# Opening of a two-layer decoder kernel: zero matmuls, order of the first norm, blocks of the model dimension, the leading tile in plain fp32

## The chip, the cores and the metric

The kernel runs as one program on one NeuronCore of a Trainium2 chip. The metric is the device time of one execution in microseconds (us), the median of several runs. TensorE (PE) multiplies matrices, VectorE (DVE) and ScalarE (ACT) do elementwise work, GpSimd (POOL) does small work, and SyncE (SP) issues most of the loads. They run side by side and meet at semaphores; each takes its own instructions in order.

## What is computed

Two pre-norm residual layers over 256 tokens of 1024 values, all in fp32. Layer 0 mixes tokens with dilated attention, layer 1 with latent attention; each then has a mixture of experts (32 experts, two for a token) and a gated embedding:

```python
for i in range(DEPTH):                      # DEPTH = 2
    h = _rmsnorm(x, norm_mix[i])
    y = _dilated_attention(h, dsa_w_in, dsa_w_out) if i == 0 else _mla(h, ...)
    x = x + y
    x = x + _hier_moe(_rmsnorm(x, norm_moe[i]), ...)
    x = x + (p[i] @ ple_w[i]) * jax.nn.sigmoid(_rmsnorm(x, norm_ple[i]) @ ple_w_gate[i])
return _rmsnorm(x, norm_final)

# in _dilated_attention: 3 groups (dilations 1, 4, 16) x (query, key, value) x 8 heads x 128
qkv = (h @ w_in).reshape(Bn, S, DSA_GROUPS, 3, DSA_HEADS, DSA_HEAD_DIM)
```

The change lies in the first norm and in the projections of head 0, the first part of `h @ w_in`.

## The kernel before

Tokens stand in two chunks of 128 (TC = 2), the model dimension in eight blocks of 128 (KD = 8). The opening goes as follows.

- SyncE loads x chunk by chunk and the identity, then the weights of heads 0 and 1 (`load_head`, L457 to L472): for each head and each of the three groups the query and the key columns (two loads of 512 KB, the three "tiles" g = 0, 1, 2), then three loads of value columns. The first load of all counts on `first_q_in`, all others on `landed_dsa`. GpSimd loads the gains (L594) and, when tile 2 of head 0 has landed, the constants, the distances and the router (L599 to L621).
- The norm: for each chunk VectorE squares one half of x and ScalarE the other (`square`, L668 and L1024), VectorE adds (L1032), ScalarE takes the root (L678), VectorE the reciprocal (L1039), and both scale a half into `hs` (L672, L1044). PE turns `hs` block by block (`turn_rows`, L1603), VectorE multiplies by the gains on the way out of PSUM into `hT` (`gains_on`, L1055).
- The weights' rows are split as "(p k)": partition p holds the rows 8p to 8p + 7. So the k-th block of `hs` takes every eighth value of x, read with a stride.
- A product of fp32 precision is made of three single-pass matmuls: high weights by high h, high weights by low h, low weights by high h. High parts are ScalarE's casts (`high_hT` L772, `high_qk` L706, `high_v` L712), low parts VectorE's subtractions (L1146, `low_qk` L1072, `low_v` L1077). The leading tile (head 0, g = 0) is done pass by pass (L1710); all others block by block (`three_pass`, L1616 to L1618, from `project_qk` and `project_v`). Other products are plain fp32 matmuls of `pe.matmul` on fp32 operands.
- The projections go to two PSUM banks in turn (`proj_bank`): tiles 0, 1, 2, then the values of chunk 0 and of chunk 1. So the values of chunk 1 write the bank of tile 2, and `project_v` waits for its copy before that chunk (`qk_copied`, 2 + c and more).
- ScalarE's order after the high part of h is written out by hand:

```python
            high_qk(0, 1, 0, first=True)
            copy_qk(0, 0, 0, first=True)
            high_qk(0, 2, 0)
            high_v(0, 0, first=True)
            copy_qk(0, 1, 0, first=True)
            high_qk(1, 0, 1)
            copy_qk(0, 2, 0, first=True)
            high_qk(1, 1, 1)
            step(0, 1, 1, first=True)
```

`high_qk` waits for the landing of its tile, `copy_qk` (L719) for the projection. From then on `step` attends to head h while it projects head h + 1: PE does the scores (L1656), tiles 0 and 1, the transposes of the softmax (L1667), tile 2, the weighted values (L1680), the values. The loads of head h + 2 wait for the slots that head h frees; the first loads of experts wait for the slots of the last heads.

## Time and profile before

| | us |
|---|---|
| median of 3 runs | 1349.45 (1346.6 to 1352.28) |
| the profiled execution | 1347.4 |
| its span in the profile | 1345.3 |
| PE busy | 1035.3 (77%) |
| VectorE busy | 454.6 (34%) |
| ScalarE busy | 298.0 (22%) |

Times in the profile are us from the span's start, of one execution. Busy shares are means over stages with different limits. Matmuls are pipelined, so the duration of one (275 ns, say) is longer than the distance between two in a row. PE is the matmuls, PEld the weight loads beside them. L12 is line 12 of the kernel. The arrow in brackets names what ended the idle time before an instruction. In order of time a row has the start, the duration, the engine, the line, the operation and its tiles. A stretch's row has its length, the busy time and count of PE, PEld, DVE, ACT and POOL, the granted clock (1.00 is the full one), the DMA engines' share and GB/s.

### The profile page before, as it was taken

The page shows a single profiled execution, that of the slowest core. Times are in us where ns is not written, and L with a number is a line of the kernel's source. Part 1 is how long each engine was busy: PE and PEld are TensorE (multiplying, and loading weights), DVE is VectorE, ACT ScalarE, POOL GpSimd, SP SyncE. Part 2 cuts the span into 40 slices and gives each one's busy share as a digit, 9 for nine tenths or more (in the row PEclk, how much of TensorE's full clock was granted, in tenths as well). Part 3 has the DMA queues.
Part 4 walks back from the last instruction along what each step waited for, and adds up shares of the span by engine and source line. Part 5 has one row for each costly group of instructions (what it writes and reads, how often), then busy time and mean ns, then how long its engine had stood idle before and what let it go on. Part 6 is the DMA issues. An engine that isn't in the chain of part 4 may idle for free.

```text
span 1345.3 us, 31101 instructions
## 1 busy us (share of the span) xinstructions
PE 1035.3 (77%) x13816; PEld 811.3 (60%) x13816; DVE 454.6 (34%) x1005; ACT 298.0 (22%) x573; POOL 16.4 (1%) x25
## 2 busy tenths in 40 slices
PE   7999999988767666656676989988667657656667
PEld 7999999965545445444454756656444444534446
DVE  5545555562212111111212775522121111212127
ACT  5433444330100000000002754311000000000007
POOL 2000000000000000000000010000000000000000
PEclk9999999999988887888888999989788898888879
DMA  9996553599999999999999950899999999999991
GB/s 283 310 256 168 160 140 125 223 384 426 425 427 425 427 427 426 426 425 426 427 426 378 390 195 1 320 422 425 426 426 427 426 425 427 427 426 425 427 374 43
DMA packets 115817, 469.94 MB, mean 349 GB/s; under 512 B 4816, under 2 KB 79696, under 8 KB 90992
## 3 DMA queue, kind: packets, MB, share of 16 engines
q1 hardware_dynamic: 115008, 465.78, 86.8%
q8 instruction: 108, 1.77, 0.5%
q0 software_dynamic: 688, 2.28, 0.4%
q14 instruction: 13, 0.11, 0.0%
HBM read 467.00 MB, written 1.05 MB: 348 GB/s over the span
## 4 chain that ended last, share of the span: by engine, by line
DMA 52%; PE 40%; DVE 4%; ACT 2%; issue 2%; DVEq 0%; SPq 0%; ACTq 0%
DMA ring<-moe_w_down 28%; DMA ring<-moe_w_gate 13%; DMA ring<-moe_w_up 11%; PE ps L1868 6%; PE ps L1617 5%; PE ps L1618 5%; PE ps L1616 5%; PE ps L1891 4%; PE ps L1730 2%; PE ps L1755 1%; PE ps L1969 1%; PE ps L1680 1%; PE ps L1656 1%; ACT g_hi L860 1%; PE ps L1921 1%
## 5 line engine op out<-in xcount | busy, mean ns | idle before, releaser
L1868 PE MATMUL ps<-ring,scr 128*32 128x128 f32 x8192 | 284.5, 298 | 146.0 <-DMA ring<-moe_w_up 100.0
L1868 PEld LDWEIGHTS ps<-ring,scr 128*32 128x32 f32 x8192 | 247.3, 120 | 185.5 <-DMA ring<-moe_w_up 111.7
L1891 PE MATMUL ps<-ring,scr 128*32 128x256 f32 x1920 | 159.8, 487 | 117.6 <-DMA ring<-moe_w_down 105.0
L1891 PEld LDWEIGHTS ps<-ring,scr 128*32 128x32 f32 x1920 | 78.1, 134 | 180.2 <-issue 123.3
L825 ACT COPY scr<-ps 32x256 f32<-32x256 f32 x128 | 46.8, 365 | 544.9 <-PE ps L1891 544.1
L1308 DVE TENSOR_TENSOR scr<-scr,ps 128x128 f32<-128x128 f32 x64 | 23.8, 371 | 422.7 <-PE ps L1868 422.7
L1321 DVE COPY scr<-ps 32x256 f32<-32x256 f32 x128 | 53.3, 417 | 243.1 <-PE ps L1891 242.3
L1616 PE MATMUL ps<-a_hT_hi,w_qk_hi 128*128 128x256 f32 x368 | 104.4, 284 | 0.0
L1618 PE MATMUL ps<-a_hT_hi,w_qk_lo 128*128 128x256 f32 x368 | 103.8, 282 | 0.0
L1617 PE MATMUL ps<-hT_lo,w_qk_hi 128*128 128x256 f32 x368 | 103.6, 282 | 0.0
L1921 PE MATMUL ps<-scr 128*128 128x512 f32 x128 | 64.6, 651 | 15.4 <-DVE scr L1321 15.4
L818 ACT ACTIVATE scr<-ps 128x128 f32<-128x128 f32 x64 | 17.8, 278 | 260.7 <-PE ps L1868 260.7
L1755 PEld LDWEIGHTS ps<-scr,hs 128*128 128x128 f32 x512 | 61.9, 198 | 17.1 <-issue 17.1
L1616 PEld LDWEIGHTS ps<-a_hT_hi,w_qk_hi 128*128 128x128 f32 x368 | 70.0, 190 | 0.0
L1618 PEld LDWEIGHTS ps<-a_hT_hi,w_qk_lo 128*128 128x128 f32 x368 | 69.7, 190 | 0.0
L1617 PEld LDWEIGHTS ps<-hT_lo,w_qk_hi 128*128 128x128 f32 x368 | 69.7, 189 | 0.0
L1072 DVE TENSOR_TENSOR w_qk_lo<-ring,w_qk_hi 128x2048 fp32r<-128x2048 f32 x24 | 54.9, 2290 | 42.7 <-ACT w_qk_hi L706 42.7
L1755 PE MATMUL ps<-scr,hs 128*128 128x128 f32 x512 | 68.0, 287 | 0.0
L1921 PEld LDWEIGHTS ps<-scr 128*128 128x128 f32 x128 | 25.1, 207 | 52.1 <-issue 26.3
L706 ACT CAST w_qk_hi<-ring 128x2048 fp32r<-128x2048 f32 x23 | 43.9, 1909 | 8.4 <-DMA ring<-dsa_w_in 8.4
L1616 PE MATMUL ps<-w_v_hi,a_hT_hi 128*128 128x384 f32 x128 | 43.4, 339 | 0.0
L1617 PE MATMUL ps<-w_v_lo,a_hT_hi 128*128 128x384 f32 x128 | 42.8, 334 | 0.0
(283 smaller groups left out, 1195.1 us busy)
## 6 DMA issues: line engine op xcount, KB each, us to landing
ring<-moe_w_gate SPq DMA_DIRECT2D x64, 2048.0 KB, 36.5
ring<-moe_w_up SPq DMA_DIRECT2D x64, 2048.0 KB, 36.4
ring<-moe_w_down SPq DMA_DIRECT2D x60, 2048.0 KB, 36.8
ring<-dsa_w_in SPq DMA_DIRECT2D x72, 512.0 KB, 6.9
ring<-ple_w_gate SPq DMA_DIRECT2D x4, 2048.0 KB, 37.0
ring<-dsa_w_out SPq DMA_DIRECT2D x2, 2048.0 KB, 13.6
scr<-moe_w_down SPq DMA_DIRECT2D x4, 1024.0 KB, 7.3
scr<-moe_w_down SPq DMA_DIRECT2D x8, 512.0 KB, 9.5
```

The source lines that it names most:

```text
L706: act.copy(w_qk_hi[(GROUPS * par + g) % 2], w_qk[par][g]).then_inc(S("w_qk_high"), 1)
L825: ins = act.copy(e_y[CW * (i % GE):CW * (i % GE) + CW, T * q:T * q + T], bank(6)[CW * q:CW * q + CW, 0:T])
L1072: dve.tensor_tensor(w_qk_lo[par][g], w_qk[par][g], w_qk_hi[(GROUPS * par + g) % 2].bitcast(F32), ALU.subtract).then_inc(S("w_qk_low"), 1)
L1321: ins = dve.tensor_copy(e_y[CW * (i % GE):CW * (i % GE) + CW, T * q:T * q + T], bank(6)[CW * q:CW * q + CW, 0:T])
L1616: pe.matmul(dst, w_hi, x_hi, start=first, stop=False)
L1617: pe.matmul(dst, w_hi, x_lo, start=False, stop=False)
L1618: return pe.matmul(dst, w_lo, x_hi, start=False, stop=last)
L1730: mm = pe.matmul(bank(mix_bank(l, c, n)), m_o[:, k, rows], tile(Tiles.MLA_OUT + n, KD, 512)[:, k, :], start=(k == 0), stop=(k == KD - 1))
L1755: mm = pe.matmul(bank(7)[:, k * P:(k + 1) * P], hs[:, c, 4 * half + k, :], e_oneh[:, c, :], start=(c == 0), stop=(c == TC - 1))
L1868: mm = pe.matmul(bank(b)[CW * q:CW * q + CW, 0:P], xT[:, k, :], tile(t, KD, FF)[:, k, P * q:P * q + P], start=(k == 0), stop=(k == KD - 1))
L1891: mm = pe.matmul(bank(6)[CW * q:CW * q + CW, 0:T], e_hT[:, CW * j:CW * j + CW], down[j][:, T * q:T * q + T], start=(j == 0), stop=(j == FF ...
L1921: mm = pe.matmul(bank(2 * c + n), e_sc[:, c * P:(c + 1) * P], e_y[:, 512 * n:512 * n + 512], start=False, stop=True, skip_group_check=True)
```

## The change

- GpSimd first fills `warm` with zeros, and PE does 16 matmuls on it while x is loading. The waits on `fills` go up by one.
- ScalarE scales the second half of chunk 0, then squares chunk 1; it scales both halves of chunk 1. VectorE scales the first half of chunk 0 only.
- The split of the weights' rows becomes "(k p)": block k is the rows 128k to 128k + 127. The scaling reads x contiguously; the gains' layout follows.
- The product of the leading tile is one plain fp32 product of `w_qk[0][0]` and `a_hT` (h in a scratch region of its own). It waits for the gains and for the landings. Its high and low parts fall away, so the counts of `w_qk_high`, `w_qk_low` and `q_high` go down by one, in all later waits too.
- Tile 1 is done pass by pass, as the leading tile was; tile 2 block by block as before. The values of head 0 are done pass by pass over both chunks: high by high, high weights by low h, low weights by high h.

```diff
--- before.py
+++ after.py
@@ -295,6 +295,8 @@
         a_o = scratch(5760, HEADS, T)
         a_pT = scratch(7808, TC * 4, P)
         a_dist = scratch(8960, TC, 4 * P)
+        a_hT = scratch(5760, KD, T)
+        warm = scratch(7808, P)
 
         ring_flat = ring[:, :, :].rearrange("p s n -> p (s n)")
 
...
@@ -421,7 +423,7 @@
         block = ctx.enter_context(nc.Block())
 
 
-        dsa_in_v = dsa_w_in.rearrange("(p k) (g w n) -> g p k w n", k=KD, g=GROUPS, w=3)
+        dsa_in_v = dsa_w_in.rearrange("(k p) (g w n) -> g p k w n", k=KD, g=GROUPS, w=3)
         ple_gate_v = [ple_w_gate[l].rearrange("(k p) (n j) -> n p k j", p=P, j=512) for l in range(2)]
         dsa_out_v = dsa_w_out.rearrange("(k p) (n j) -> n p k j", p=P, j=512)
         mla_out_v = mla_w_out.rearrange("(k p) (n j) -> n p k j", p=P, j=512)
...
@@ -591,6 +593,7 @@
 
         @block.gpsimd
         def _(pool):
+            pool.memset(warm, 0.0).then_inc(S("fills"), 1)
             pool.dma_start(wts[:, :], gains).then_inc(S("wts_in"), 16)
             pool.memset(gp8, -BIG).then_inc(S("fills"), 1)
             pool.memset(ones, 1.0).then_inc(S("fills"), 1)
...
@@ -762,25 +765,37 @@
                     act.wait_ge(S("o_copied"), HEADS - 1)
                     act.copy(a_o_hi[:, 0:HEADS - 1, :], a_o[:, 0:HEADS - 1, :]).then_inc(S("o_high"), 1)
 
-            act.wait_ge(S("fills"), 2)
+            act.wait_ge(S("fills"), 3)
             table(ACT.Sqrt)
-            for c in range(TC):
-                norm_chunk(0, c)
+
+            def first_root(c):
+
+                square(0, c)
+                act.wait_ge(S("var_ready"), c + 1)
+                act.activation(root[:, c:c + 1], root[:, c:c + 1], ACT.Sqrt, scale=1.0 / D).then_inc(S("root_ready"), 1)
+                act.wait_ge(S("rstd_ready"), c + 1)
+
+            def first_scale(c, b):
+                return act.activation(hs[:, c, 4 * b:4 * b + 4, :],
+                                      x_sb[:, c, 512 * b:512 * b + 512].rearrange("p (k t) -> p k t", t=P),
+                                      ACT.Copy, scale=rstd[:, c:c + 1])
+
+            first_root(0)
+            first_scale(0, 1).then_inc(S("hs_a"), 1)
+            first_root(1)
+            first_scale(1, 0).then_inc(S("hs_d"), 1)
+            first_scale(1, 1).then_inc(S("hs_a"), 1)
+
             def high_hT(c, b):
                 act.wait_ge(S("hT_ready"), 2 * c + b + 1)
                 blocks = slice(4 * b, 4 * b + 4)
-                return act.copy(by_chunk(a_hT_hi[:, blocks, :], c), by_chunk(hT[:, blocks, :], c))
-
-            act.wait_ge(S("hT_turned"), 2)
+                return act.copy(by_chunk(a_hT_hi[:, blocks, :], c), by_chunk(a_hT[:, blocks, :], c))
+
+            act.wait_ge(S("hT_turned"), 4)
             high_hT(0, 0)
-            act.wait_ge(S("first_q_in"), 16)
-            act.copy(w_qk_hi[0][:, :, 0:DH], w_qk[0][0][:, :, 0:DH]).then_inc(S("q_high"), 1)
-            act.wait_ge(S("hT_turned"), 4)
             high_hT(0, 1).then_inc(S("hT_high"), 1)
             high_hT(1, 0)
             high_hT(1, 1).then_inc(S("hT_high"), 1)
-            act.wait_ge(landed_dsa[0], 16)
-            act.copy(w_qk_hi[0][:, :, DH:2 * DH], w_qk[0][0][:, :, DH:2 * DH]).then_inc(S("w_qk_high"), 1)
             high_qk(0, 1, 0, first=True)
             copy_qk(0, 0, 0, first=True)
             high_qk(0, 2, 0)
...
@@ -1052,7 +1067,7 @@
                 for b in range(2):
                     dve.wait_ge(S("hT_turned"), 4 * i + 2 * c + b + 1)
                     if i == 0:
-                        dve.tensor_tensor(by_class(hT[:, 4 * b:4 * b + 4, :], c),
+                        dve.tensor_tensor(by_class(a_hT[:, 4 * b:4 * b + 4, :], c),
                                           bank(4 + 2 * c + b, 4, P).rearrange("p k (i r) -> p k r i", r=CLASSES),
                                           gain[:, 4 * b:4 * b + 4].unsqueeze(2).unsqueeze(3).to_broadcast(
                                               [P, 4, CLASSES, P // CLASSES]), ALU.mult).then_inc(S("hT_ready"), 1)
...
@@ -1132,10 +1147,12 @@
                                       a_o_hi[:, 0:HEADS - 1, :].bitcast(F32), ALU.subtract).then_inc(S("o_low"), 1)
                 copy_v(h_proj, buf, first)
 
-            for c in range(TC):
-                square(0, c)
-                roots(0, c, c + 1)
-                scale(0, c)
+            square(0, 0)
+            roots(0, 0, 1)
+            dve.tensor_scalar(hs[:, 0, 0:4, :], x_sb[:, 0, 0:512].rearrange("p (k t) -> p k t", t=P), rstd[:, 0:1], None,
+                              ALU.mult).then_inc(S("hs_d"), 1)
+            square(0, 1)
+            roots(0, 1, 2)
             for c in range(TC):
                 gains_on(0, c)
             for c in range(TC):
...
@@ -1143,10 +1160,10 @@
                 dve.wait_ge(S("hT_high"), c + 1)
                 for b in range(2):
                     blocks = slice(4 * b, 4 * b + 4)
-                    ins = dve.tensor_tensor(by_chunk(hT_lo[:, blocks, :], c), by_chunk(hT[:, blocks, :], c),
+                    ins = dve.tensor_tensor(by_chunk(hT_lo[:, blocks, :], c), by_chunk(a_hT[:, blocks, :], c),
                                             by_chunk(a_hT_hi[:, blocks, :].bitcast(F32), c), ALU.subtract)
                 ins.then_inc(S("hT_low"), 1)
-            for g in range(GROUPS):
+            for g in range(1, GROUPS):
                 low_qk(0, g, 0)
             low_v(0, 0)
             low_qk(1, 0, 1)
...
@@ -1619,7 +1636,7 @@
 
             def project_qk(h, g, buf, first=False):
 
-                pe.wait_ge(S("w_qk_low"), GROUPS * h + g + 1)
+                pe.wait_ge(S("w_qk_low"), GROUPS * h + g)
 
                 if g == 2:
                     pe.wait_ge(S("qk_copied"), GROUPS * h + 1)
...
@@ -1690,31 +1707,53 @@
                 weigh(h_att, 1 - buf, first)
                 project_v(h_proj, buf)
 
+            pe.wait_ge(S("fills"), 1)
+            for _ in range(16):
+                pe.matmul(bank(3)[:, 0:P], warm, warm, start=True, stop=True)
             for c in range(TC):
                 turn_rows(0, c)
 
+            pe.wait_ge(S("first_q_in"), 16)
+            for which in range(2):
+                if which == 1:
+                    pe.wait_ge(landed_dsa[0], 16)
+                for k in range(KD):
+                    if which == 0 and k % 4 == 0:
+                        pe.wait_ge(S("hT_ready"), TC + 1 + k // 4)
+                    mm = pe.matmul(bank(proj_bank(0, 0))[:, which * T:which * T + T], w_qk[0][0][:, k, which * DH:(which + 1) * DH],
+                                   a_hT[:, k, :], start=(which == 0 and k == 0), stop=(k == KD - 1), skip_group_check=True)
+            mm.then_inc(S("qk_ready"), 1)
 
             pe.wait_ge(S("hT_high"), TC)
-            pe.wait_ge(S("q_high"), 1)
-            for w, h in ((w_qk_hi[0], a_hT_hi), (w_qk_hi[0], hT_lo), (w_qk_lo[0][0], a_hT_hi)):
+            pe.wait_ge(S("w_qk_high"), 1)
+            for w, h in ((w_qk_hi[1], a_hT_hi), (w_qk_hi[1], hT_lo), (w_qk_lo[0][1], a_hT_hi)):
                 if h is hT_lo:
                     pe.wait_ge(S("hT_low"), TC)
-                if w is not w_qk_hi[0]:
+                if w is not w_qk_hi[1]:
                     pe.wait_ge(S("w_qk_low"), 1)
                 for which in range(2):
-                    if w is w_qk_hi[0] and h is a_hT_hi and which == 1:
-                        pe.wait_ge(S("w_qk_high"), 1)
                     for k in range(KD):
-                        first = w is w_qk_hi[0] and h is a_hT_hi and which == 0 and k == 0
-                        last = w is not w_qk_hi[0] and k == KD - 1
-                        mm = pe.matmul(bank(proj_bank(0, 0))[:, which * T:which * T + T],
+                        first = w is w_qk_hi[1] and h is a_hT_hi and which == 0 and k == 0
+                        last = w is not w_qk_hi[1] and k == KD - 1
+                        mm = pe.matmul(bank(proj_bank(0, 1))[:, which * T:which * T + T],
                                        w[:, k, which * DH:(which + 1) * DH],
                                        h[:, k, :], start=first, stop=last,
                                        skip_group_check=True)
             mm.then_inc(S("qk_ready"), 1)
-            for g in range(1, GROUPS):
-                project_qk(0, g, 0, first=True)
-            project_v(0, 0)
+            project_qk(0, 2, 0, first=True)
+            pe.wait_ge(S("w_v_high"), 1)
+            for w, h in ((w_v_hi, a_hT_hi), (w_v_hi, hT_lo), (w_v_lo[0], a_hT_hi)):
+                if w is not w_v_hi:
+                    pe.wait_ge(S("w_v_low"), 1)
+                for c in range(TC):
+                    if w is w_v_hi and h is a_hT_hi:
+                        pe.wait_ge(S("qk_copied"), 2 + c)
+                    for k in range(KD):
+                        mm = pe.matmul(bank(proj_bank(0, GROUPS + c))[:, 0:GROUPS * DH], h[:, k, c * P:(c + 1) * P], w[:, k, :],
+                                       start=(w is w_v_hi and h is a_hT_hi and k == 0), stop=(w is not w_v_hi and k == KD - 1),
+                                       skip_group_check=True)
+                    if w is not w_v_hi:
+                        mm.then_inc(S("v_ready"), 1)
             step(0, 1, 1, first=True)
             with pe.Fori(0, HEADS // 2 - 1) as it:
                 step(2 * it + 1, 2 * it + 2, 0)
...
@@ -2222,7 +2261,7 @@
         "distances": distance_table(),
 
         "gains": np.ascontiguousarray(np.concatenate(
-            [g.reshape(KD, P).T if n % 3 == 2 or n == 3 else g.reshape(P, KD) for n, g in enumerate(gains)]
+            [g.reshape(KD, P).T if n % 3 == 2 or n % 3 == 0 else g.reshape(P, KD) for n, g in enumerate(gains)]
             + [a["mla_q_norm"].reshape(-1, P).T, a["mla_kv_norm"].reshape(-1, P).T]
             + [a["norm_moe"][l].reshape(KD, P).T for l in range(2)], axis=1)),
         "routers": np.stack([r.reshape(KD, P, NR).transpose(1, 0, 2).reshape(P, KD * NR) for r in routers]),
```

## Rows read from the trace of the kernel before

**Rows 1.** The page's slices: 40 equal parts of the span, tenths busy, and GB/s moved.
```profile
PE   7999999988767666656676989988667657656667
...
GB/s 283 310 256 168 160 140 125 223 384 426 425 427 425 427 427 426 426 425 426 427 426 378 390 195 1 320 422 425 426 426 427 426 425 427 427 426 425 427 374 43
```

**Rows 2.** Busy us by stretch: the end of the opening, and the attention.
```profile
14.00:17.80 3.80, 3.80 (x22) 3.80 (x21) 3.80 (x3) 1.90 (x1) 0.00 (x0) 0.55 1.07 266
40.00:270.00 230.00, 230.00 (x1707) 226.12 (x1706) 126.34 (x142) 94.24 (x101) 0.00 (x0) 1.00 0.65 196
```

**Rows 3.** The chain that ended last, 180 to 345 us: start, us, what.
```profile
219.39 1.75 PE ps L1656 x12
...
249.19 1.75 PE ps L1656 x12
```

**Rows 4.** SyncE in order of time: a first load of experts.
```profile
249.22 0.33 SPq L497 DMA_DIRECT2D ring<-moe_w_gate  x1
```

**Rows 5.** The first scores in time order; then the readers of `w_v_hi`, 20 to 45 us.
```profile
40.02 1.92 PE L1656 MATMUL ps<-scr 128*128 128x256 f32 x12
...
L1616 PE MATMUL ps<-w_v_hi,a_hT_hi x16: 334/334/339, 31.7 to 39.5; 128*128 128x384 f32 x16
L1077 DVE TENSOR_TENSOR w_v_lo<-ring,w_v_hi x1: 3358/3358/3358, 26.5 to 26.5; 128x3072 fp32r<-128x3072 f32 x1
```

**Rows 6.** The chain that ended last, 0 to 60 us.
```profile
12.96 7.49 PE ps L1710 x48
```

**Rows 7.** All engines in order of time, 0 to 21 us: start, us, instruction.
```profile
1.26 0.66 POOL L594 DMA_DIRECT2D wts<-gains  x1 [0.81 <-POOLq L2236]
...
5.83 1.24 ACT L672 ACTIVATE hs<-x_sb,small 128x512 f32<-128x512 f32 x1 [0.23 <-DVE small L1039]
...
8.21 0.16 DVE L1039 RECIPROCAL small<-small 128x1 f32<-128x1 f32 x1 [0.27 <-ACT small L678]
...
9.01 2.83 DVE L1055 TENSOR_TENSOR hT<-ps,wts 128x512 f32<-128x512 f32 x4
...
14.02 1.90 ACT L706 CAST w_qk_hi<-ring 128x2048 fp32r<-128x2048 f32 x1 [0.17 <-DMA ring<-dsa_w_in]
...
15.40 3.13 PE L1710 MATMUL ps<-hT_lo,w_qk_hi 128*128 128x256 f32 x16
...
20.28 0.28 PE L1616 MATMUL ps<-a_hT_hi,w_qk_hi 128*128 128x256 f32 x1
```

**Rows 8.** ScalarE in order of time, 23 to 80 us.
```profile
23.72 2.77 ACT L712 CAST w_v_hi<-ring 128x3072 fp32r<-128x3072 f32 x1 [0.85 <-DMA ring<-dsa_w_in]
...
30.04 1.90 ACT L706 CAST w_qk_hi<-ring 128x2048 fp32r<-128x2048 f32 x1 [3.07 <-DMA ring<-dsa_w_in]
31.89 0.59 ACT L719 COPY scr<-ps 128x512 f32<-128x512 f32 x1
33.42 1.92 ACT L706 CAST w_qk_hi<-ring 128x2048 fp32r<-128x2048 f32 x1 [0.94 <-DMA ring<-dsa_w_in]
...
57.95 1.91 ACT L706 CAST w_qk_hi<-ring 128x2048 fp32r<-128x2048 f32 x1 [3.49 <-DMA ring<-dsa_w_in]
```

**Rows 9.** The scores' matmuls: of all heads by form, then of head 0 (40 to 42).
```profile
L1656 PE MATMUL ps<-scr 128*128 128x256 f32 x32 | 9.5, 379 | 0.0
...
L1656 PE MATMUL ps<-scr x12: 273/275/382, 40.0 to 41.7; 128*128 128x128 f32 x8, 128*128 128x256 f32 x4
```

**Rows 10.** Loads: the gains; then the first two weight loads with their landing.
```profile
wts<-gains POOLq DMA_DIRECT2D x1, 33.5 KB, 4.6
...
L464 SPq DMA_DIRECT2D ring<-dsa_w_in x2: 669/737/805, 2.1 to 2.9; - x2
...
DMA to landing us min/median/max: 6.4/7.0/7.5
```

**Rows 11.** Transposes, by line: ns min/median/max, first and last start.
```profile
L1603 PE MATMUL ps<-cst,hs x16: 414/421/476, 6.7 to 10.7; 128*128 128x128 f32 x16
...
L1610 PE MATMUL ps<-cst,x_sb x80: 272/273/332, 272.0 to 1314.5; 128*128 128x128 f32 x80
```

**Rows 12.** The page's groups: VectorE's subtraction for a tile of queries and keys.
```profile
L1072 DVE TENSOR_TENSOR w_qk_lo<-ring,w_qk_hi 128x2048 fp32r<-128x2048 f32 x24 | 54.9, 2290 | 42.7 <-ACT w_qk_hi L706 42.7
```

More of the change, by code:

```diff
@@ L1069, in low_qk @@
             def low_qk(h, g, par):
-                dve.wait_ge(S("w_qk_high"), GROUPS * h + g + 1)
+                dve.wait_ge(S("w_qk_high"), GROUPS * h + g)
                 dve.tensor_tensor(w_qk_lo[par][g], w_qk[par][g],
@@ L1461, in low_queries @@
             def low_queries(n):
-                dve.wait_ge(S("w_qk_high"), GROUPS * HEADS + n + 1)
+                dve.wait_ge(S("w_qk_high"), GROUPS * HEADS + n)
                 cols = slice(512 * n, 512 * n + 512)
@@ L1507, in lat_gains @@
                 dve.tensor_scalar(m_kvT[:, cols], bank(3)[:, cols], kvg, None, ALU.mult).then_inc(S("lnT_copied"), 1)
-                dve.wait_ge(S("q_high"), c + 2)
+                dve.wait_ge(S("q_high"), c + 1)
                 dve.tensor_tensor(m_ql_lo[:, :, cols], m_qlT[:, :, cols], m_ql_hi[:, :, cols].bitcast(F32),
@@ L2041, in project_q @@
             def project_q(c, ns):
-                pe.wait_ge(S("q_high"), c + 2)
-                pe.wait_ge(S("w_qk_low"), GROUPS * HEADS + ns[-1] + 1)
+                pe.wait_ge(S("q_high"), c + 1)
+                pe.wait_ge(S("w_qk_low"), GROUPS * HEADS + ns[-1])
                 b = 4 if c == 0 else 0
```

## The prediction

> **What bounds the kernel now.** I read the page's slices first [rows 1]: TensorE is full from slice 2 to slice 8, where the memory moves 125 to 310 GB/s; from slice 9 on it moves some 425 GB/s and TensorE is half idle. The stretch from 40 to 270 us says it in us [rows 2]: PE is busy 230.00 of 230.00 us in the attention layer. One head takes 29.8 us there: the scores of two heads in turn start at 219.39 and 249.19 us [rows 3], and an expert load is issued at 249.22 us, when a projection ends [rows 4]. So a time won or lost before 40 us moves the rest of the attention, the expert loads, their stream and the end by as much, as far as PE stays the bound from 40 us on. The milestone to forecast is the start of the first scores, 40.02 us [rows 5].
>
> Up to there the chain goes: x lands; squares and roots; gains; the high part of h; 48 matmuls of the leading tile, from 12.96 us for 7.49 [rows 6]; 96 matmuls of tiles 1 and 2 from 20.28 [rows 7]; 48 value matmuls from 31.7 [rows 5], without a gap. That PE shows no gap does not make it the only limit: a few us beside it run the landings of the weights and ScalarE's casts, which wait for them. ScalarE's casts start at 14.02 [rows 7], 23.72, 30.04 and 33.42 [rows 8], each as its weights land; the one at 30.04 (head 1's first tile) had waited 3.07 us. A faster opening meets these next.
>
> **The change, part by part.**
> *Zeros.* 16 plain fp32 products of 128 columns are 32 records: a plain product leaves two (8 heads with 2 products of 256 columns stand as x32 [rows 9]). PE can start when Pool has filled `warm`, about 1.5 us (Pool's first own instruction stands at 1.26 [rows 7]). The gains load behind that fill is issued some 0.2 us later; it takes 4.6 us to land [rows 10], so 6.1, and is wanted at 7.8: hidden. A record of 128 columns costs 0.11 us at the full clock (half of the 0.22 below), twice that at the lower level. Which level holds? The opening's transposes take 414 to 476 ns each, later ones 272 to 273 [rows 11]: the opening runs at the lower of the two levels (1.2 GHz), although the profile prints 1.00 there. All 32 at the low level end at 1.5 + 32 x 0.22 = 8.5 us; raised half way, at 6.8. The transposes stand behind them on PE, and could begin at about 6.5. I take 7.
>
> *Scaling and chunk 1.* ScalarE's half of the scaling, read with a stride, costs 1.24 us [rows 7]; a pass of the same size without one costs 0.59 (the copy at 31.89 [rows 8]). Both are bounds; I take 0.62, as the operand is contiguous now. So ScalarE squares chunk 1 some 0.6 us sooner, and the second root's reciprocal ends at 7.8 in place of 8.37 [rows 7]. ScalarE scales both halves of chunk 1 (until 8.4 and 9.0); VectorE, free of that, takes the four gains back to back, 2.83 us [rows 7], from 7.8 to 10.6, where they ran to 11.84. With zeros until 8.5 the gains run from 9.2 to 12.0.
>
> *The leading tile in plain fp32.* It starts with the third gain, at 9.9 (11.3 with late zeros), and needs no high or low part. Its weights have landed: issues at 2.1 and 2.9 us land after 6.4 and 7.5, so at 8.5 and 10.4 [rows 10], the second wanted half way through. 48 single-pass matmuls become 32 records of 256 columns. Price: a head's scores are 4 records of 256 and 8 of 128 columns, 2048 columns in all, in 1.92 us with the last one's own 0.27, 1.65 without [rows 5, 9]; so 0.21 to 0.24 us per 256. I take 0.22: 7.0 us. That is more PE time than three passes at full speed (96 records from 20.28 to 31.7, 0.119 each, 48 are 5.7 us) and a little less than the 7.49 that the three passes took. It ends at 16.9. At the low level throughout it is 14 us, and the end 24. In this trace the clock fell to a mean of 0.55 between 14 and 17.8 us [rows 2], after PE had been idle from 11.1 (the last transpose) to 12.96, and a pass of 16 matmuls took 3.13 us [rows 7] in place of 1.9. The gaps that are left among the transposes are of that order; the same fall once more costs what it cost there, 1.2 us in that pass and some 0.3 beside it: 18.4.
>
> *Tiles 1 and 2.* ScalarE loses the cast of a tile and VectorE the subtraction (2.29 us [rows 12]). Tile 1 lands at 14.02 as now; cast (1.90) to 15.9, low part to 18.2. PE wants these at 16.9 and, for the third pass, at 20.7: hidden. Tile 2 is cast behind `copy_qk(0, 0)`, by 19.8, low part by 22.1; PE wants it at 22.6: hidden, by little. The 96 matmuls take 11.4 us, so PE reaches the values at 28.3 in place of 31.7.
>
> *Values by passes.* Here the gain meets its cover. The values land at 23.7, cast to 26.5, low part to 29.9 [rows 5, 8]: both in time. The first pass of chunk 0 (8 matmuls; 48 took 40.02 - 31.7 = 8.3 us, so 8 take 1.38) runs from 28.3 to 29.7. But chunk 1 writes the bank of tile 2, and its first pass waits for `copy_qk(0, 2)`. On ScalarE this copy stands behind the cast of head 1's first tile, which waits for its landing until 30.04 and ends at 31.9; the copy runs from 31.89 to 32.48 [rows 8]. Before, chunk 1 was not wanted until 31.7 + 4.1 = 35.8 us, so the copy was hidden; the new order wants it at 29.7. PE stands for 2.8 us, and five groups of 8 are left: 32.5 + 5 x 1.38 = 39.4. The scores start at 39.4 in place of 40.02: **0.6 us**. This is so for every end of the leading tile up to 32.5 - 1.4 - 11.4 = 19.7 us; beyond, each us costs one, and the break-even is 20.3. So the fall of the clock (18.4) changes nothing at the end, nor do late zeros alone (18.3).
>
> *Contiguous blocks of the model dimension.* The weights' packets are runs of 512 B as before and as many; only which row goes to which partition changes. I take the landings unchanged; the trace bounds it poorly: runs of 512 B move at 266 GB/s in the stretch of [rows 2] with the DMA share above 1, so there is no idle time to win, and no load of 512 B runs in the new order. I allow 10% either way.
>
> From 40 us on I find no further wait: ScalarE's second cast of head 1 ends at 35.3, its subtraction before 38, and PE wants it at 46; the next landing that it waits for ends at 57.95 [rows 8], for head 2, which PE wants past 70. So 0.6 us passes through: the profiled execution from 1347.4 (span 1345.3 and 2.1 around it) to 1346.8, and the median of the three runs from 1349.45, 2.05 above it, to 1348.8. The three runs spread over 5.7 us, 0.4%; a change of 0.5% (6.7 us) is about what a measurement of this kernel can tell from none.
>
> **The rivals.**
> *A, the landing gives way* (15%). If head 1's first tile lands earlier, the copy comes earlier, at most until PE itself is the limit: 29.7 in place of 32.5. Gain 0.6 + 2.8 = 3.4 us: 1346.0. For it: neighbouring partitions read 288 KB apart until now, and 36 KB apart after. Against: the DMA share above 1, which the order does not touch.
> *B, the landing comes later, and the kernel is slower* (10%). The eight rows of one partition now lie 4.5 MB apart instead of side by side. If the head loads slow down by a share f, the landing at 30.04 moves by f x 27.9 us (it counts from the first issue, 2.15), and PE's end with it, one for one. It decides from f = 2% on: 10% gives 2.8 - 0.6 = 2.2 us more (1351.6), 25% gives 6.4 (1355.8). For it: no row shows this order with such runs. Against: the same rows are read, in all.
> The Trainium skill, "DMA: Bandwidth & Descriptors", section "Latency and other measured facts", reports copies at half rate where the rows of neighbouring partitions lie large powers of two apart, cured by a few KB of padding. Neither 288 KB nor 36 KB is such a distance, and the 4.5 MB step lies within a partition; by that rule B does not happen. No row here shows it.
> *C, the leading tile is late, slower too* (13%). Zeros until 8.5 and the lower level over most of the plain product: 11.3 + 10 to 14 = 21 to 25 us against the 20.3. Price 1 to 5 us: 1350.5 to 1354.5. For it: the opening is at the low level already, and the plain product has the most to lose. Against: PE works from 1.5 us where it did nothing until 6.7 [rows 11].
> *The change doesn't do what it says*: the zeros raise nothing and hold the transposes. That is C's first half, and alone it costs nothing at 40 us.
>
> **How the numbers follow.** Forecast (a gain of 0.3 to 1.2 us) 62%, A 15%, C 13%, B 10%. Likeliest 1348.8. The range takes in A's whole gain and most of C's loss, with the 2 us by which a median of such runs lies off: 1343.3 to 1353.0; B beyond 15% is left out. Faster by over 0.5% needs 6.7 us, twice what A can give: 4%, for what I have not seen. Slower by over 0.5% is B from 26% on, or B with C: 5%. Within: 91%.
>
> **What would show it.** Zeros from 1.5 to about 7 us; later transposes near 272 ns; gains done by 10.6; 32 plain records from 9.9 to 17 or 19; in the values, between the first two groups of 8, a PE gap of 2 to 3 us that ScalarE's copy of the product ends at 32.5; scores at 39.4; the cast of head 1's first tile still at 30.0. No gap and an earlier cast: A. A cast later than 30.7: B. A plain product that ends past 20.3: C. I am wrong altogether if the scores come 2 us or more sooner with the landing unmoved, or if what is won by 40 us does not reach the end.

## The result, and the profile after

| | before | after |
|---|---|---|
| median of 17 runs each | 1347.62 us (1346.58 to 1352.28) | 1353.89 us (1350.89 to 1355.99) |
| the profiled execution | 1347.4 | 1353.1 |
| its span | 1345.3 | 1351.1 |

The ratio is 1.0042, with a 95% interval from 1.0035 to 1.0049: the change makes the kernel slower by some 5.7 us. The forecast was 1348.8, with a range up to 1353.0; the cause of the loss does not stand in its working.

Is the loss in the opening? PE in order of time, after (start, us, instruction; in brackets the idle time before it and what ended it):

```profile
1.00 5.74 PE L1712 MATMUL ps<-scr 128*128 128x128 f32 x32 [1.00 <-POOL scr L596]
6.63 1.06 PE L1620 MATMUL ps<-cst,hs 128*128 128x128 f32 x8
8.84 1.27 PE L1620 MATMUL ps<-cst,hs 128*128 128x128 f32 x8 [1.14 <-ACT hs L779]
10.44 7.14 PE L1723 MATMUL ps<-scr,ring 128*128 128x256 f32 x32 [0.33 <-DVE scr L1070]
17.24 2.23 PE L1738 MATMUL ps<-a_hT_hi,w_qk_hi 128*128 128x256 f32 x16
...
29.21 1.65 PE L1752 MATMUL ps<-w_v_hi,a_hT_hi 128*128 128x384 f32 x8 [0.19 <-ACT scr L722]
32.74 1.50 PE L1752 MATMUL ps<-w_v_hi,a_hT_hi 128*128 128x384 f32 x7 [1.88 <-ACT scr L722]
```

and ScalarE in the same view:

```profile
25.83 2.76 ACT L715 CAST w_v_hi<-ring 128x3072 fp32r<-128x3072 f32 x1 [5.80 <-DMA ring<-dsa_w_in]
28.50 0.58 ACT L722 COPY scr<-ps 128x512 f32<-128x512 f32 x1
30.31 1.90 ACT L709 CAST w_qk_hi<-ring 128x2048 fp32r<-128x2048 f32 x1 [1.24 <-DMA ring<-dsa_w_in]
32.12 0.58 ACT L722 COPY scr<-ps 128x512 f32<-128x512 f32 x1
```

The opening is what the forecast drew: zeros, quick transposes, a plain product that ends at 17.6, and a stop of PE between the first two groups of the values, until the copy that stands behind head 1's cast. The scores start at 39.82 (40.02 in [rows 5]), and by 249 us 0.23 us are still won:

```profile
248.96 1.75 PE ps L1673 x12
```

(249.19 in [rows 3]). At 290.12 the next milestone stands (before, 290.35). So the loss lies behind the attention. Walking down PE's rows, the two traces part behind the last expert of layer 0. First before, then after:

```profile
731.98 3.70 PE L1921 MATMUL ps<-scr 128*128 128x512 f32 x8 [0.96 <-DVE scr L1321]
735.52 2.04 PE L1610 MATMUL ps<-cst,x_sb 128*128 128x128 f32 x16
737.32 1.24 PE L1969 MATMUL ps<-g_hi,hT_hi 128*128 128x512 f32 x4
```

```profile
733.30 3.70 PE L1960 MATMUL ps<-scr 128*128 128x512 f32 x8 [0.97 <-DVE scr L1338]
736.84 1.04 PE L1627 MATMUL ps<-cst,x_sb 128*128 128x128 f32 x8
740.69 1.09 PE L1627 MATMUL ps<-cst,x_sb 128*128 128x128 f32 x8 [2.81 <-issue]
```

The change touches none of these lines. 16 transposes (`turn_x`, behind the expert loop) run without a break before; after, PE stands for 2.81 us in their middle. "issue" means that nothing which the profile shows held it: no semaphore, no landing. (The gap stands where PE waits for the second chunk of `x_sb`, but the two copies that it waits for end at 737.73 and 737.63.) The chain that ended last passes through it, so it counts in full:

```profile
737.01 0.87 PE ps L1627 x8
737.88 2.81 issue
740.69 0.67 PE ps L1627 x4
```

Layer 1 has the same gap in the same place, and none before:

```profile
1317.29 1.04 PE L1627 MATMUL ps<-cst,x_sb 128*128 128x128 f32 x8
1319.49 1.10 PE L1627 MATMUL ps<-cst,x_sb 128*128 128x128 f32 x8 [1.16 <-issue]
```

What fills no semaphore and no data queue may be the engine's own code. The page counts its transfers apart, as packets of the kind "instruction" (queue, packets, MB, share); before, then after:

```profile
q8 instruction: 108, 1.77, 0.5%
```

```profile
q8 instruction: 109, 1.79, 0.5%
```

1.77 MB over 108 packets are 16 KB each. PE's compiled program is a file of 15592 instructions of 64 bytes before and of 15627 after, so a packet is 256 of them, and the change adds 35. The Trainium skill, "Runtime: NRT & Kernel Launch", section "The launch sequence", says of instructions that their fetch runs by itself, ahead, with no instruction for it; these rows agree that it is a transfer of its own, and the gaps are where it did not come far enough ahead.

The trace has the time of each packet too. After, none of these starts between 725 and 738.1 us; the next one falls within the gap. The view of 738.1 to 740.69 us has it:

```profile
q8 instruction: 1, 0.02, 2.6%
```

It starts at 738.21 and takes 1.06 us, and PE goes on at 740.69.

**The theory (blocks).** PE's code comes in blocks of 256 instructions. Behind each expert loop PE jumps over the branch for overflowing experts, which is never taken. The next block is asked for only about when this one is entered, so what counts is how many instructions are left between the place where the jump lands and the end of that block.

Where do the blocks end? "Place" is an instruction's number in the compiled file, modulo 256. The loops and jumps of the file, followed through, give 13816 matmuls before, as many as the trace has records, so each record can be given its number. In the unrolled experts of layer 0, before, the issue gaps of 2.45 us ahead of 323.29 and of 0.67 ahead of 346.27 fall at instructions 3572 and 4340, both at place 244. In layer 1's experts they fall at place 250. Between the two the file has six labels, marks for its loops and jumps. So the labels count in the file but not in the blocks; every further label moves the end one place on: 250 behind layer 0's loop, 256 behind layer 1's. (The expectations below count to 244 or to 256 in both layers, and so are off by up to 12.)

By this count 53 instructions are left behind the jump before, in both layers, and 18 after. These 18 are a wait, eight transposes of two instructions each, and the wait for the second chunk: PE runs dry exactly where the gap stands, in layer 0 and in layer 1. With 53 left it has passed the 16 transposes and stands for ScalarE's casts anyway (0.37 us ahead of 738.93).

**The rivals.** *Opening*: the earlier start or the new order of the weights' rows disturbs the memory or the clock later on. *More code*: each added instruction costs, wherever it lies. *Clock*: the last expert ran at the lower level after the change (its 32 products took 3.49 us at a granted clock of 0.54, in place of 1.93 at 1.00), which is why the scatter (L1960) starts 1.3 us later.

### The profile page after: what moved, and what is told of

Its sections match the earlier page's. It is cut to its first block, busy times and chain, and to the rows that moved or that the text cites. A ratio compares the mean times of both kernels' runs of the same rounds, so it can differ in the third digit from the quotient of the medians.

```text
span 1351.1 us, 31137 instructions
## 1 busy us (share of the span) xinstructions
PE 1041.4 (77%) x13832; PEld 817.1 (60%) x13832; DVE 452.1 (33%) x1003; ACT 296.1 (22%) x572; POOL 13.6 (1%) x26
## 4 chain that ended last, share of the span: by engine, by line
DMA 49%; PE 41%; DVE 4%; issue 2%; ACT 1%; SPq 1%; DVEq 0%; ACTq 0%
DMA ring<-moe_w_down 33%; DMA ring<-moe_w_gate 8%; DMA ring<-moe_w_up 7%; PE ps L1907 6%; PE ps L1930 5%; PE ps L1634 5%; PE ps L1635 5%; PE ps L1633 5%; PE ps L1769 2%; PE ps L1794 2%; PE ps L1960 2%; PE ps L2008 1%; PE ps L1697 1%; PE ps L1673 1%; DMA ring<-dsa_w_in 1%
## 5 line engine op out<-in xcount | busy, mean ns | idle before, releaser
L1907 PE MATMUL ps<-ring,scr 128*32 128x128 f32 x8192 | 280.8, 296 | 140.7 <-DMA ring<-moe_w_up 92.5
L1930 PE MATMUL ps<-ring,scr 128*32 128x256 f32 x1920 | 164.6, 501 | 122.5 <-DMA ring<-moe_w_down 109.2
L1633 PE MATMUL ps<-a_hT_hi,w_qk_hi 128*128 128x256 f32 x352 | 99.9, 284 | 0.0
L1635 PE MATMUL ps<-a_hT_hi,w_qk_lo 128*128 128x256 f32 x352 | 99.2, 282 | 0.0
L1634 PE MATMUL ps<-hT_lo,w_qk_hi 128*128 128x256 f32 x352 | 99.1, 282 | 0.0
L1794 PEld LDWEIGHTS ps<-scr,hs 128*128 128x128 f32 x512 | 68.7, 216 | 19.4 <-issue 19.4
L1794 PE MATMUL ps<-scr,hs 128*128 128x128 f32 x512 | 74.8, 305 | 0.0
L833 ACT ACTIVATE scr<-ps 128x128 f32<-128x128 f32 x64 | 17.8, 278 | 257.6 <-PE ps L1907 257.6
L1960 PE MATMUL ps<-scr 128*128 128x512 f32 x128 | 59.2, 605 | 15.8 <-DVE scr L1338 15.8
L1960 PEld LDWEIGHTS ps<-scr 128*128 128x128 f32 x128 | 23.0, 189 | 48.6 <-DVE scr L1338 25.6
L1291 DVE TENSOR_TENSOR scr<-ps,wts 128x512 f32<-128x512 f32 x36 | 24.9, 692 | 47.7 <-PE ps L1794 44.8
L1633 PE MATMUL ps<-w_v_hi,a_hT_hi 128*128 128x384 f32 x112 | 38.1, 340 | 0.0
```

The lines of the kernel that those rows point to most:

```text
L1633: pe.matmul(dst, w_hi, x_hi, start=first, stop=False)
L1634: pe.matmul(dst, w_hi, x_lo, start=False, stop=False)
L1635: return pe.matmul(dst, w_lo, x_hi, start=False, stop=last)
L1794: mm = pe.matmul(bank(7)[:, k * P:(k + 1) * P], hs[:, c, 4 * half + k, :], e_oneh[:, c, :], start=(c == 0), stop=(c == TC - 1))
L1907: mm = pe.matmul(bank(b)[CW * q:CW * q + CW, 0:P], xT[:, k, :], tile(t, KD, FF)[:, k, P * q:P * q + P], start=(k == 0), stop=(k == KD - 1))
L1930: mm = pe.matmul(bank(6)[CW * q:CW * q + CW, 0:T], e_hT[:, CW * j:CW * j + CW], down[j][:, T * q:T * q + T], start=(j == 0), stop=(j == FF ...
```

## The experiments

A measure for all of them: from the start of the scatter of layer 0 (731.98 before) to the end of the span. It holds both turns and the stream between them, and none of the opening. "Left" is the number of instructions from the jump's target to the end of its block, the same in both layers; 14 "in" means that the target is the 15th instruction of the next block.

| kernel | left | scatter to end, us | ratio to before, 95% |
|---|---|---|---|
| before | 53 | 613.3 | |
| after | 18 | 617.8 | 1.0042 (1.0035 to 1.0049) |
| b_pad35 | 18 | 619.2 | 1.0046 (1.0032 to 1.0061) |
| b_ifpad35 | 18 | 617.9 | 1.0037 (1.0024 to 1.0050) |
| a_pad32 | 14 in | 621.4 | 1.0039 (1.0025 to 1.0053) |
| a_ifpad32 | 14 in | 615.4 | 1.0050 (1.0035 to 1.0065) |
| a_ifpad32_copy | 14 in | 619.4 | 1.0047 (1.0029 to 1.0066) |
| b_pad17 | 36 | 613.4 | 1.0003 (0.9991 to 1.0016) |
| b_shift256 | 53 | 613.0 | 1.0001 (0.9992 to 1.0010) |
| b_layout | 53 | 613.3 | 0.9993 (0.9982 to 1.0005) |
| a_z8 | 50 | 612.8 | 1.0000 (0.9988 to 1.0012) |
| a_z8_copy | 50 | 612.9 | 0.9987 (0.9975 to 0.9998) |
| a_w4_copy | 52 | 612.7 | 0.9984 (0.9973 to 0.9995) |
| a_w4_copy_np | 66 | 613.6 | 0.9982 (0.9972 to 0.9992) |

The packets show the cause in each of these traces. In layer 0 the one behind the jump starts 4.6 to 5.0 us after the scatter in all 14 kernels. Where PE stands for it, it goes on 2.4 to 2.7 us after the packet's start, in both layers:

| kernel, layer | scatter | packet (length) | PE goes on | from packet's start |
|---|---|---|---|---|
| after, 0 | 733.30 | 738.21 (1.06) | 740.69 | 2.48 |
| b_pad35, 0 | 732.99 | 737.76 (0.91) | 740.28 | 2.52 |
| b_ifpad35, 0 | 735.06 | 740.10 (1.06) | 742.50 | 2.40 |
| a_pad32, 0 | 735.04 | 739.81 (1.01) | 742.49 | 2.68 |
| a_ifpad32, 0 | 733.11 | 737.78 (1.07) | 740.41 | 2.63 |
| a_ifpad32_copy, 0 | 731.90 | 736.52 (0.99) | 739.18 | 2.66 |
| b_pad17, 0 | 734.43 | 739.31 (1.13) | 741.72 | 2.41 |
| after, 1 | 1313.75 | 1316.92 (1.07) | 1319.49 | 2.57 |
| b_ifpad35, 1 | 1314.27 | 1318.82 (1.08) | 1321.38 | 2.56 |

So in layer 0 the block is there 7.3 to 7.5 us after the scatter, and what PE can do without it until then decides how long it stands.

**b_pad35: nothing but 35 instructions.** Waits that are already met, ahead of PE's first transposes, in the kernel before:

```diff
+            for _ in range(71):
+                pe.wait_ge(S("fills"), 1)
             for c in range(TC):
                 turn_rows(0, c)
```

> The kernel before with 71 waits on a semaphore value that is already reached, ahead of PE's first transposes: 35 more instructions in PE's program, as many as the change adds, and nothing else. Code-position theory: the two gaps that stand before the transposes behind each expert loop in the changed kernel (2.81 and about 1.2 us, ended by nothing but issue) appear here too, since PE's instructions seem to come in blocks of 256 and the place behind the expert loop now lies 13 and 7 instructions ahead of a block's end; 1351 to 1354 us where before has 1347.6. Opening theory (the slow part comes from the new opening: zeros, layout, its clock): no change, within 0.1%. The first scores stay at 40.0 us in both.

The scores start at 40.16, so the opening is untouched, and the whole loss is there. Its trace shows the gaps too:

```profile
732.99 5.55 PE L1923 MATMUL ps<-scr 128*128 128x512 f32 x8 [0.95 <-DVE scr L1321]
738.38 1.04 PE L1610 MATMUL ps<-cst,x_sb 128*128 128x128 f32 x8
740.28 1.09 PE L1610 MATMUL ps<-cst,x_sb 128*128 128x128 f32 x8 [0.86 <-issue]
```

The scatter took 5.55 us in place of 3.70 (granted clock 0.52 from 732 to 737) and the gap is shorter by about as much: PE comes later to a block that arrives at its own time, 7.29 us after the scatter (7.39 in after). The loss needs nothing of the change's opening, which refutes "opening".

**a_z8: the change, 32 instructions shorter.** A zero product is four instructions; eight of the 16 are dropped:

```diff
-            for _ in range(16):
+            for _ in range(8):
                 pe.matmul(bank(3)[:, 0:P], warm, warm, start=True, stop=True)
```

> The changed kernel with 8 zero products in place of 16: 32 instructions fewer on PE, 3 more than before the change. Code-position theory: both gaps go, 1348 to 1350 us, and what is left over the kernel before is the 1.3 us of the last expert if that is something else. Opening theory: 1353 to 1355, as the opening is the same but for the zeros, whose end (6.7 us) was no limit. First scores 39.8 us in both.

The scores start at 39.83 as in after, 16 transposes stand in one row at 735.38, and the loss is gone: the whole of it hung on 32 instructions whose result is not used.

**a_z8_copy: and the copy ahead of the cast.** On top, tile 2's copy comes before head 1's cast on ScalarE:

```diff
             copy_qk(0, 1, 0, first=True)
-            high_qk(1, 0, 1)
             copy_qk(0, 2, 0, first=True)
+            high_qk(1, 0, 1)
```

> As the one with 8 zero products, and ScalarE's copy of tile 2 of head 0 moved ahead of its cast of head 1's first tile. If the wait that ends at 32.7 us in the changed kernel is this copy's, standing behind a cast that waits for its landing, PE goes on at about 30.5 and the next limit is the low part of the values (32.0 us in the changed kernel's trace): scores at 37.2 to 37.6 in place of 39.8, and 2.2 to 2.6 us less than with 8 zeros alone: 1345.5 to 1347.5 by the code-position theory. If the landing of the weights is itself the limit and not the order on ScalarE: no change against 8 zeros alone.

The values run without a gap from 30.95, so the wait was the copy's. But the scores start at 39.28 and not by 37.6, since the plain product of the profiled execution took 8.97 us in place of 7.14 (granted clock 0.77 from 10 to 19.7). The median is 2.2 us under that of a_z8 (1345.76 for 1347.97), as expected.

**b_layout: only the order of the rows.** Before, with "(k p)", the contiguous scaling and the gains' layout:

```diff
-        dsa_in_v = dsa_w_in.rearrange("(p k) (g w n) -> g p k w n", k=KD, g=GROUPS, w=3)
+        dsa_in_v = dsa_w_in.rearrange("(k p) (g w n) -> g p k w n", k=KD, g=GROUPS, w=3)
```

> The kernel before with only the blocks of the model dimension contiguous (weights' rows split the new way, scaling and gains to match); PE's program has the same length. Code-position theory: 1347 to 1348, no gap behind the experts; scaling at 0.7 in place of 1.24 us on ScalarE, scores at 39.5 to 40.0. Rival B of the prediction (the new row order slows the loads): landings of head 1's first tile clearly past 30.3 us. In the changed kernel that cast started at 30.31 (30.04 before) but the values' cast at 25.83 (23.72 before); if this is the layout's doing, the values' cast starts past 25 here too.

```profile
23.04 2.78 ACT L713 CAST w_v_hi<-ring 128x3072 fp32r<-128x3072 f32 x1 [2.26 <-DMA ring<-dsa_w_in]
25.70 0.59 ACT L720 COPY scr<-ps 128x512 f32<-128x512 f32 x1
29.93 1.91 ACT L707 CAST w_qk_hi<-ring 128x2048 fp32r<-128x2048 f32 x1 [3.64 <-DMA ring<-dsa_w_in]
```

Against 23.72 and 30.04 in [rows 8] nothing lands later. The scores start at 38.48, 1.5 us sooner and 1.0 sooner than expected: the leading tile starts at 12.34 for 12.96, and its three passes take 6.0 us in place of 7.49, as the fall of the clock in [rows 2] stayed away. The ratio does not show that this gain reaches the end (0.9982 to 1.0005).

**b_ifpad35: 35 instructions that are never run.** The waits stand within the branch that is jumped over in layer 0, so every instruction up to the loop's end keeps its place:

```diff
                     pe.wait_ge(S(f"o_x{l}"), 2)
+                    for _ in range(70 if l == 0 else 0):
+                        pe.wait_ge(S("fills"), 1)
```

> The kernel before with the same 35 instructions added on PE, but inside layer 0's branch for overflowing experts, which is jumped over and never runs: the opening, the attention and layer 0's expert loops keep their places, only what stands behind the first expert loop moves (and with it all of layer 1). Code-position theory, the place behind the loop: the gap before the second eight transposes in layer 0 (about 2.8 us) and in layer 1 (1.2) are there, 1351 to 1352.5. If what matters is where the loops' bodies lie, layer 0 loses nothing and layer 1 some 1.5 to 2. If added instructions cost by being run at the opening: no change.

```profile
738.60 1.04 PE L1610 MATMUL ps<-cst,x_sb 128*128 128x128 f32 x8
742.50 1.09 PE L1610 MATMUL ps<-cst,x_sb 128*128 128x128 f32 x8 [2.87 <-issue]
```

Code that PE never runs costs what the change costs (1353.16, where 1351 to 1352.5 was expected). Only the place of what lies behind it can be the cause. The scores start at 41.84 in this execution, which the measure from the scatter leaves out.

**a_ifpad32, a_ifpad32_copy, a_pad32: the target pushed into the next block.** After with 32 more instructions, in the same branch (64 waits), the same with the copy moved, and 64 waits ahead of the zeros instead:

> The changed kernel with 32 instructions more inside the same branch that never runs: the place behind layer 0's expert loop goes from 13 instructions ahead of a multiple of 244 + 256 n to 237 ahead, behind layer 1's from 7 to 231. Code-position theory: both gaps go, 1349 to 1350.5 where the changed kernel has 1353.9; what is left over 1347.4 is the share of the loop bodies' places in layer 0. Any theory that puts the loss in the opening: 1353.9.

> As the one before (changed kernel, 32 instructions in the branch that never runs, all 16 zero products), and ScalarE's copy of tile 2 ahead of the cast of head 1's first tile. The run with 8 zeros reached its scores at 39.28 because the plain product of the leading tile ended at 19.7 (17.6 with 16 zeros); with 16 zeros I expect the values to start at 28.9 to 29.1, their low part at about 32 and scores at 37.2 to 37.6, and a time 2 to 2.5 us under the one with the padding alone. If instead the product is as slow again: 39.3.

> The changed kernel with the 32 instructions at the opening of PE (64 waits on a value already reached, ahead of the zeros) in place of the branch: the places behind the loops are as in the run with them in the branch, the loops' bodies of layer 0 lie 32 further on. Code-position theory: no gap before the transposes; 1348 to 1350.5. The zeros start some 1 us later (about 2.5), end at 8, which the slack of the opening takes: scores at 39.8.

My expectation for all three, that the gap would go, failed (medians 1355.58, 1354.26 and 1353.37). The gap moved ahead of all transposes:

```profile
733.11 3.70 PE L1960 MATMUL ps<-scr 128*128 128x512 f32 x8 [0.97 <-DVE scr L1338]
740.41 1.94 PE L1627 MATMUL ps<-cst,x_sb 128*128 128x128 f32 x16 [3.60 <-issue]
```

I had thought of the block's end as a line to be cleared. But beyond it the target itself lies in a block that is not there, and PE waits for it as long (3.60 us; 3.57 in a_ifpad32_copy). The single runs of a_ifpad32 lie at 1350.2 to 1350.6 and at 1355.2 to 1356.2; the profiled one is of the first kind, and has no gap in layer 1, where a_ifpad32_copy has 2.53 us. There its packet starts 0.7 us after the scatter (1313.16), and 3.6 us after it in a_ifpad32_copy (1316.14); why is open. The zeros of a_pad32 start at 4.47, not at 2.5, and its scores at 39.62 all the same. The scores of a_ifpad32_copy start at 37.13: the copy's order is worth 2.7 us at 40 us.

**b_pad17: how far from the end is enough.** Before with 35 waits, 17 instructions:

> Before with 17 more PE instructions ahead of its first transposes; the jump behind the expert loop still starts in the block it started in (place 248 of 256), the target is at 213. Blocks of 256: no gap or under 0.5 us, 1347.6 to 1348.2. Rival, that the loss grows with the instructions added (35 gave 5 to 6 us): 1350.3.

```profile
734.43 3.70 PE L1923 MATMUL ps<-scr 128*128 128x512 f32 x8 [0.96 <-DVE scr L1321]
737.97 2.04 PE L1610 MATMUL ps<-cst,x_sb 128*128 128x128 f32 x16
...
1314.94 2.04 PE L1610 MATMUL ps<-cst,x_sb 128*128 128x128 f32 x16
1317.87 0.39 PE L1971 MATMUL ps<-g_hi,hT_hi 128*128 128x512 f32 x1 [0.89 <-issue]
```

With 36 left a gap is there in both layers, against my expectation, but it falls behind the transposes, beside the wait for the casts. In layer 0 the profile puts it down to ScalarE: PE stands for 1.72 us until 741.72, where its first gate product could have started near 739.8 (in b_shift256, with nearly the same scatter, it starts at 739.64). By VectorE's rows this is 0.65 us from 764 to 877 us, which the experts' stream then takes up. From the scatter of layer 1 to the end it costs 0.3 us (36.4 for 36.1). The loss does not grow in step with the number of instructions: 17 cost nothing clear of noise. And the scatter starts at 734.43, 2.4 us later than before, in a kernel that is no slower: this start varies from 730.3 to 734.4 among the eight kernels without a loss, so the 1.3 us of after are within what one execution differs from the next.

**b_shift256: more code, the same places.** The first block product of each bank is done three times, in experts 4 to 7 of layer 0's first pass (only the last counts), where PE waits for the memory:

```diff
-                                mm = pe.matmul(bank(b)[CW * q:CW * q + CW, 0:P], xT[:, k, :],
-                                               tile(t, KD, FF)[:, k, P * q:P * q + P],
-                                               start=(k == 0), stop=(k == KD - 1))
+                                for again in ((1, 1, 0) if k == 0 and first and l == 0 and i >= 4 else (0,)):
+                                    mm = pe.matmul(bank(b)[CW * q:CW * q + CW, 0:P], xT[:, k, :],
+                                                   tile(t, KD, FF)[:, k, P * q:P * q + P],
+                                                   start=(k == 0), stop=(again == 1 or k == KD - 1))
```

> Before, with 64 products repeated (256 instructions of PE) in experts 4 to 7 of layer 0's first pass, where PE waits for the memory: all behind them lies 256 instructions later, at the same places within blocks of 256. Blocks of 256: no issue gap in the transposes at 735.5 and 1312.8 (under 0.3 us), time as before, 1347.6 +-0.7. Rival, that more code or a farther jump is what costs: a gap of 2 us or more at one turn, 1350 or more.

```profile
q8 instruction: 109, 1.79, 0.5%
```

```profile
729.83 3.51 PE L1892 MATMUL ps<-ring,scr 128*32 128x256 f32 x32 [2.71 <-DMA ring<-moe_w_down]
734.31 3.70 PE L1922 MATMUL ps<-scr 128*128 128x512 f32 x8 [0.97 <-DVE scr L1321]
737.84 2.04 PE L1610 MATMUL ps<-cst,x_sb 128*128 128x128 f32 x16
```

256 instructions and one packet more, no gap and no loss, where 35 cost 6 us. This refutes "more code" and agrees with a period of 256. Its last expert ran at the lower level (3.51 us), as after's did, and it is no slower, which refutes "clock" as the cause. More closely: counted from the scatter, VectorE's rows in the kernels with 50 or more left agree with those of before within 0.15 us up to 877 us, where after is 3.2 us late.

**a_w4_copy, a_w4_copy_np: the change with its code put back.** Four zero products of 512 columns in place of 16 of 128 and the copy moved, with 27 waits (code one instruction behind its old place) and without (13 ahead of it):

```diff
-            for _ in range(16):
-                pe.matmul(bank(3)[:, 0:P], warm, warm, start=True, stop=True)
+            for _ in range(27):
+                pe.wait_ge(S("fills"), 1)
+            for _ in range(4):
+                pe.matmul(bank(3), warm[:, 0:P], warm, start=True, stop=True)
```

> After with 4 zero products of 512 columns in place of 16 of 128 and 27 waits ahead of them, so that PE's code lies one instruction from where it lay before; and the copy of tile 2 before head 1's first cast. Scores at 37.7 (PE no longer stands for the copy), no issue gap in the transposes behind the loops, time 1345.3 (1344.5 to 1346.3), ratio 0.9983. Rival, that what is won at the opening is lost to the memory later whatever the code's place: 1347 or more.

> The same without the 27 waits: code 13 instructions before its old place; jump targets at 183 and 189 of 256, loop heads at 242 and 247, just ahead of an edge. If only the jumps out of the loops matter: scores 37.7, no gap at the transposes, 1345.3. If the place of the loop heads matters too, three passes each a gap of 0.5 to 3 us, up to 1350.

Both are faster than before, by their ratios 2.2 and 2.4 us, and so than after (medians 1346.39 and 1345.29 against 1348.04 of before on the same chip). The scores of the first start at 38.09, those of the second at 37.14. In the second the loops' heads lie just ahead of a block's end, and the third and fourth pass of layer 0 begin with long gaps:

```profile
502.08 6.44 PE L1907 MATMUL ps<-ring,scr 128*32 128x128 f32 x128 [6.54 <-issue]
623.33 5.51 PE L1907 MATMUL ps<-ring,scr 128*32 128x128 f32 x127 [8.43 <-issue]
```

(Before has 2.67 and 2.74 us there.) They cost nothing: there the memory sets the pace and PE catches up. So it is not the stall that costs but where it stands.

## Why the prediction was wrong, point by point

- *Zeros*: right. The transposes behind them start at 6.63 (taken 7), and they raised the level: eight transposes take 1.06 us where they took 1.94, 414 ns each, in [rows 11].
- *Scaling and gains*: right within 0.3 us: 0.72 for 0.62, the gains done at 10.9 for 10.6.
- *The leading tile*: right. 32 records in 6.8 us from start to start, 0.21 each (taken 0.22), ending at 17.6 for 16.9. The fall of the clock of [rows 2] stayed away in this execution (1.00 from 14 to 17.8); a_z8_copy's 8.97 shows that it can come back. In after's order a late end is covered, as worked out: in a_pad32 the product ends at 20.0 and the scores start at 39.62. With the copy moved it is not (39.28 for 37.13).
- *Landings*: right for head 1's first tile (30.31 for 30.04). The values of head 0 landed at 25.83 and not 23.7, which cost 0.19 us. This landing lies between 23.0 and 26.2 among the kernels with the new order, so the order is not its cause.
- *Values by passes*: the mechanism is right to the row, PE's stop at the copy, which ends at 32.74 for 32.5. PE stood for 1.88 us and not 2.8, as it came to the values at 29.21 and not 28.3. The five groups left take 7.08 us, 1.42 each, in place of 1.38. Scores 39.82 for 39.4, gain 0.2 for 0.6.
- *Rival A*, *B*, *C*: none came. B is refuted by b_layout, as the rule of the Trainium skill that the prediction quotes had it ("DMA: Bandwidth & Descriptors", "Latency and other measured facts"). A's price holds when the copy no longer waits: 2.7 us at 40 us where 2.8 was worked out, and some of it shows at the end (a_z8_copy, a_w4_copy).
- *"From 40 us on I find no further wait ... So 0.6 us passes through"*: this step failed. The 0.2 us did pass through to 290 us, and then 4.5 us were lost from the scatter on (613.3 to 617.8), 4.1 of them at the gaps behind the two expert loops. I looked for what the change does to data, queues and semaphores, and took code at nothing. But it adds 35 instructions to PE, and every later instruction of PE lies 35 further on. The trace of before had the warning: issue gaps of 2.45 and 0.67 us at 323 and 346 us, in a stretch where PE waits for nothing that is shown. I read PE only up to 290 us.

The sum now, by how much later after reaches the same row: -0.23 at 290 us; +1.32 at the scatter of layer 0 (within the spread of single executions); +4.20 where the first casts behind it are used (738.26 to 742.46), so 2.88 for the gap; +4.51 at the scatter of layer 1 (1309.24 to 1313.75); +5.75 behind its gap (1316.18 to 1321.93), so 1.24; +5.8 at the end. What stays open: the medians differ by 6.3 us, and the losses by ratio go up to 0.5%, more than the 4.5 of this one profile. b_pad35 and a_pad32 lose 5.9 and 8.1 in theirs; 1.7 of it, in each, are eight products that take 5.38 and 5.35 us in place of 3.68 (from 855.49 and 858.59), at a granted clock of 0.68. Why the clock falls there, and in their scatter, I don't know. The rows show when a packet starts, not what asks for it: that this is the entry into the block before is inferred.

## What to carry to other kernels

An edit of an unrolled program moves all the code behind it, so compare "issue" gaps on the chain after each edit, not only where the edit is, and look first behind long loops and jumps, where the code does not run straight on. A change that wins 1 or 2 us is judged only once the code lies where it lay: a few satisfied waits, or fewer and wider dummy matmuls, put it back. And when a copy frees a bank for the next product, keep it ahead of any cast that still waits for a landing.

## What the runs showed of the hardware that I had not expected

- PE's code arrives in packets of 16 KB, 256 instructions, labels not counted. A packet takes 0.9 to 1.1 us in these stretches, and PE goes on 2.4 to 2.7 us after its start. The stops are 0.9 to 3.6 us long behind layer 0's loop (in after the memory moves 367 GB/s meanwhile), and 0.9 to 2.8 behind layer 1's.
- In the attention of layer 0, before, no packet of q8 starts between 121 and 263 us, though its loop of 945 instructions is run three times: this loop's code was not fetched again.
- 35 instructions that are never run cost 0.37% (b_ifpad35); 256 that are run cost nothing measurable (b_shift256).
- A wait that is already met takes half an instruction's place (70 for 35) and some 0.05 us: 64 of them move the zeros from 1.00 to 4.47 us.
- The same 32 products of the last expert take 1.93 us in some executions (granted clock 1.00) and some 3.5 in others (0.54 to 0.56). b_shift256 had the slow ones and is no slower by its median.
